# The final norm's row sums taken from the feature tiles instead of the turned tiles, with one root for all tokens

## The chip, the cores and the metric

The kernel runs on one core of one Trainium2 chip. The metric is the device time of one execution in microseconds (us), as the median of several runs. A profiled execution is one more run, with a trace; its span goes from the first to the last instruction.

## What is computed

One decoder layer on 512 tokens of width 1024 (attention with three dilated windows, then a gated ConvFFN), everything in float32, followed by a last RMSNorm over each token's 1024 features. Only the end matters here:

```python
def rms_norm(x, gain):
    xf = x.astype(jnp.float32)
    y = xf * lax.rsqrt(jnp.mean(xf * xf, axis=-1, keepdims=True) + EPS)
    return (y * gain.astype(jnp.float32)).astype(x.dtype)
...
        x = x + g2[:, None, :] * conv_ffn(h, ffn_w_up[i], ffn_conv_w[i], ffn_conv_b[i], ffn_w_down[i])
    return rms_norm(x, norm_final)
```

## The kernel before

The residual `xT` lies turned in SBUF: 8 tiles of 128 features (partitions) by 512 tokens. The down projection is the last large product. It runs over 22 strips of the hidden width, and for every strip over the 8 output tiles `o`; each output tile has a PSUM bank of its own, `y_bank(o)`. Each product is made of three passes with split operands (`wl` with `act_h`, `wh` with `act_h`, `wh` with `act_l`). The order of all instructions on every engine is written out by hand, and semaphores alone tie the engines together.

**TensorE's tail.** The last two strips are taken tile by tile (L1047 to L1049), so that output tile 0 is done first and tile 7 last; each counts up `y_done`. Between the tiles stand the turns back: `BACK_AT` says behind which tile which turned tile `m` is made. Turned tile `m` has 128 tokens (token group `m % 4`) and 512 features (half `m // 4`), and goes into `y_bank(m)`, which is free by then. It takes four 128x128 transposes (L1055). Turned tiles 0 to 3 (features 0 to 511) stand behind tiles 4, 5 and 6; turned tiles 4 to 7 all stand behind tile 7, since they need `xT` tile 7: 4 and 5 its first 256 tokens, 6 and 7 its last 256.

**VectorE's tail.** `add_ffn(o)` (L1775) adds tile `o` to `xT` (`x2_done`), tile 7 in two halves of 256 tokens. `add_gain(m)` (L1793) multiplies turned tiles 0 to 3 with the gain row `nfin` into `out_n`, without the root. `last_root(pair)` (L1783 to L1788) makes the root of two token groups; `output(m)` (L1798) multiplies turned tiles 4 to 7 with root and gain at once.

**ScalarE's tail.** For each turned tile `m` one Square with a row sum (L1312, `ssq_o`), which needs the tile turned; after turned tiles 5 and 7 a square root of two columns (L1318); last, `out_n` parts 2 and 3 are scaled by their root (L1323). GpSimd does the same for parts 0 and 1 (L680).

**The stores.** All eight stores of 128 tokens by 512 features (256 KB each) are issued by SyncE (L619) in the order 4, 0, 5, 1, 6, 2, 7, 3, each after a wait for its part; then SyncE waits until all have landed.

So the token groups 0 and 1 get their root as soon as turned tiles 4 and 5 are squared, and groups 2 and 3 get theirs in a second round.

Of the kernel before, what the change touches and what calls it, by code (L numbers as in the profile page):

```python
# [21 lines left out]
ACT = mybir.ActivationFunctionType  # L22
# [58 lines left out]
def decoder_layer(nc, x, c, w_ada, b_ada, norm_mix, norm_ffn, attn_w_in, attn_w_out,  # L81
# [11 lines left out]
    with ctx:  # L93
        def tensor(scope, name, shape, dt=F32):
            return scope.enter_context(nc.sbuf_tensor(name, shape, dt))

        def sem(name):
            return ctx.enter_context(nc.semaphore(name))
# [23 lines left out]
        ssq_o = tensor(ctx, "ssq_o", [P, NT, 2])  # L122


        scope_a = ExitStack()
# [63 lines left out]
        scope_e = ExitStack()  # L189
        out_n = tensor(scope_e, "out_n", [P, NT, D])  # L190
        nfin = tensor(scope_e, "nfin", [P, D])
        scope_e.close()

        banks = [ctx.enter_context(nc.psum_tensor(f"bank{i}", [P, T], F32)) for i in range(8)]
# [51 lines left out]
        x2_done, nat_done, ssq_done, rstd_step, out_done, root_o_done, stored = (  # L246
            sem("x2_done"), sem("nat_done"), sem("ssq_done"), sem("rstd_step"), sem("out_done"),
            sem("root_o_done"), sem("stored"))
        out_pool_done = sem("out_pool_done")
        gained, out_a_done = sem("gained"), sem("out_a_done")  # L250

        block = ctx.enter_context(nc.Block())
# [243 lines left out]
        def _(sp):  # L496
# [116 lines left out]
                sp.dma_start(down_raw(k % FRING).rearrange("p t n -> p (t n)"), w_down[k]).then_inc(fraw_in[k % FRING], 16)  # L613
            sp.wait_ge(prod_done, PRODUCTS * (FT - PLAIN))
            sp.dma_start(nfin[:], norm_final.partition_broadcast(P)).then_inc(nfin_in, 16)
            for i in range(NT):
                for m, done, value in ((i + NT, out_done, i + 1), (i, (out_pool_done, out_a_done)[i // 2], i % 2 + 1)):
                    sp.wait_ge(done, value)
                    sp.dma_start(out_rows[i][:, T * (m // 4):T * (m // 4 + 1)], out_part(out_n, m)).then_inc(stored, 16)  # L619
            sp.wait_ge(stored, 16 * 2 * NT)  # L620


# [1 line left out]
        def _(pool):  # L624
# [44 lines left out]
            for f in range(PLAIN + 1, FT):  # L669
                w = f % 2  # L670
                one, two = up_raw(w)
                for a, other_block, came in ((0, two[:, HK:KT], fraw_in[2 * w + 1]), (1, one[:, 0:HK], fraw_in[2 * w])):
                    pool.wait_ge(sum_in[w][a], 16 * sum_uses(f))
                    pool.wait_ge(came, loads_of(f, w, None))
                    nc.gpsimd.dma_start(sums[:, 4 * w + 2 * a], other_block, accum_op=ALU.add).then_inc(sum_added[w][a], 16)

            pool.wait_ge(gained, 2)
            pool.wait_ge(rstd_step, 3)
# [7 lines left out]
        def _(pe):  # L686
# [357 lines left out]
            for o in range(KT):  # L1044
                for k in (FT - 2, FT - 1):
                    slot = k % FRING
                    nc.tensor.matmul(y_bank(o)[:], wl[:, slot, o], act_h[:, slot], start=False, stop=False)  # L1047
                    nc.tensor.matmul(y_bank(o)[:], wh[:, slot, o], act_h[:, slot], start=False, stop=False)
                    last = nc.tensor.matmul(y_bank(o)[:], wh[:, slot, o], act_l[:, slot], start=False, stop=(k == FT - 1))  # L1049
                last.then_inc(y_done, 1)  # L1050
                for m in BACK_AT.get(o, ()):

                    pe.wait_ge(x2_done, 4 if m < 4 else KT if m < 6 else KT + 1)
                    for q in range(4):
                        last = nc.tensor.transpose(y_bank(m)[:, P * q:P * (q + 1)],  # L1055
                                                   xT[:, 4 * (m // 4) + q, P * (m % 4):P * (m % 4 + 1)], ident[:])
                    last.then_inc(nat_done, 1)
# [3 lines left out]
        def _(act):  # L1061
# [244 lines left out]
            downs(act, down)  # L1306

            nc.scalar.activation(warm[:, 1:2], ones[:, 0:1], ACT.Sqrt)
            for m in range(2 * NT):
                act.wait_ge(nat_done, m + 1)  # L1310

                nc.scalar.activation(out_part(out_n, m), y_bank(m)[:], ACT.Square,  # L1312
                                     accum_out=ssq_o[:, m % 4, m // 4:m // 4 + 1]).then_inc(ssq_done, 1)
                if m in (5, 7):
                    pair = (m - 5) // 2
                    act.wait_ge(rstd_step, 2 + 3 * pair)
                    lo = 2 * NT + 2 * pair
                    nc.scalar.activation(root[:, 2, lo:lo + 2], root[:, 1, lo:lo + 2], ACT.Sqrt).then_inc(root_o_done, 1)  # L1318
            for i in (2, 3):

                act.wait_ge(gained, NT)
                act.wait_ge(rstd_step, 6)
                nc.scalar.activation(out_part(out_n, i), out_part(out_n, i), ACT.Copy,  # L1323
                                     scale=root[:, ROOT_STEPS, 2 * NT + i:2 * NT + i + 1]).then_inc(out_a_done, 1)


        @block.vector
        def _(dve):
# [449 lines left out]
            def last_root(pair):  # L1778

                lo = 2 * NT + 2 * pair  # L1780
                at = slice(2 * pair, 2 * pair + 2)
                dve.wait_ge(ssq_done, NT + 2 * (pair + 1))
                nc.vector.tensor_tensor(root[:, 0, lo:lo + 2], ssq_o[:, at, 0], ssq_o[:, at, 1], ALU.add).then_inc(rstd_step, 1)  # L1783
                dve.wait_ge(rstd_step, 3 * pair + 1)
                nc.vector.tensor_scalar(root[:, 1, lo:lo + 2], root[:, 0, lo:lo + 2], 1.0 / D, EPS, ALU.mult, ALU.add
                                        ).then_inc(rstd_step, 1)
                dve.wait_ge(root_o_done, pair + 1)
                nc.vector.reciprocal(root[:, ROOT_STEPS, lo:lo + 2], root[:, 2, lo:lo + 2]).then_inc(rstd_step, 1)  # L1788
                dve.wait_ge(rstd_step, 3 * pair + 3)

            def add_gain(m):
                dve.wait_ge(ssq_done, m + 1)
# [3 lines left out]
            def output(m):  # L1796

                nc.vector.scalar_tensor_tensor(out_part(out_n, m), y_bank(m)[:],  # L1798
                                               root[:, ROOT_STEPS, 2 * NT + m % 4:2 * NT + m % 4 + 1],
                                               nfin[:, T * (m // 4):T * (m // 4 + 1)], ALU.mult, ALU.mult  # L1800
                                               ).then_inc(out_done, 1)
# [40 lines left out]
```

## Time and profile before

| | before |
|---|---|
| median of 3 runs | 950.43 us (950.26 to 952.1) |
| the profiled execution | 950.68 us, its span 948.9 us |
| TensorE busy in the span | 925.9 us (98%) |
| VectorE, ScalarE, GpSimd busy | 577.3, 445.7, 51.3 us |
| mean granted TensorE clock | 0.996 |

The busy shares average over stages of very different kinds. TensorE is never idle for long until the last product of output tile 7 starts at 937.08 us; behind that come 11.8 us in which the other engines and the stores set the time.

### The profile page before, as it was taken

Reading aid. Unit: us, or ns where it says so; the run is one execution under the profiler, and the core shown is the slowest. Engines: PE = TensorE matmul, PEld = TensorE weight load, DVE = VectorE, ACT = ScalarE, POOL = GpSimd, SP = SyncE. Lnnn points to the kernel's source line nnn. Section 1 sums busy time; section 2 is a strip of 40 time slices with the busy share of each in tenths; the row PEclk is TensorE's granted clock in tenths of the full one; section 3 lists DMA queues with packets and bytes.
Section 4 is the critical chain, followed back from the end, with each engine's and each line's share of the span. In section 5 each row is a group of like instructions: output and inputs, shape, how many; then the busy total and the mean of one; then the engine's idle time right before and its main releaser. Section 6 shows DMA issues by size and latency. Waiting matters only on the chain.

```text
span 948.9 us, 16326 instructions
## 1 busy us (share of the span) xinstructions
PE 925.9 (98%) x5828; PEld 796.2 (84%) x5828; DVE 577.3 (61%) x1269; ACT 445.7 (47%) x804; POOL 51.3 (5%) x75
## 2 busy tenths in 40 slices
PE   8999999999999999999999999999999999999996
PEld 6688887888888888888888779789999999888884
DVE  3445565736736557357365657798888888633325
ACT  7244534435444445353443445655656666523222
POOL 2000000000000000000000000411211111000000
PEclk9999999999999999999999999999999999999999
DMA  9865341443324324334142103278888885532302
GB/s 303 254 191 164 111 134 47 132 133 111 120 79 132 111 58 130 121 111 146 53 134 81 54 26 98 77 163 191 185 181 193 185 199 144 166 101 88 111 1 89
DMA packets 166516, 121.19 MB, mean 128 GB/s; under 512 B 4662, under 2 KB 149198, under 8 KB 166478
## 3 DMA queue, kind: packets, MB, share of 16 engines
q1 hardware_dynamic: 161088, 111.17, 39.1%
q0 software_dynamic: 5184, 9.44, 6.7%
q8 instruction: 23, 0.38, 0.2%
q14 instruction: 15, 0.12, 0.0%
q10 hardware_dynamic: 206, 0.08, 0.0%
HBM read 109.13 MB, written 2.10 MB: 117 GB/s over the span
## 4 chain that ended last, share of the span: by engine, by line
PE 89%; DVE 5%; ACT 2%; POOL 1%; DMA 1%; issue 1%; SPq 1%; DVEq 0%; ACTq 0%
PE bank L781 14%; PE bank L783 13%; PE bank L782 13%; PE bank L986 7%; PE bank L989 6%; PE bank L988 6%; PE bank L1035 4%; PE bank L1037 4%; PE bank L1036 4%; PE bank L863 3%; PE bank L839 3%; PE bank L806 1%; PE bank L799 1%; PE bank L821 1%; PE bank L872 1%; PE bank L874 1%
## 5 line engine op out<-in xcount | busy, mean ns | idle before, releaser
L1382 DVE TENSOR_TENSOR wl<-raw,wh 128x1024 fp32r<-128x1024 f32 (+1 forms) x127 | 150.1, 1183 | 168.6 <-ACT wh L1093 168.0
L781 PE MATMUL bank<-hh,wl 128*128 128x512 f32 x544 | 218.1, 401 | 0.0
L783 PE MATMUL bank<-hl,wh 128*128 128x512 f32 x544 | 212.4, 390 | 0.0
L782 PE MATMUL bank<-hh,wh 128*128 128x512 f32 x544 | 212.0, 390 | 0.0
L1093 ACT ACTIVATE wh<-raw 128x1024 fp32r<-128x1024 f32 (+1 forms) x127 | 130.2, 1026 | 63.3 <-PE bank L1037 50.9
L781 PEld LDWEIGHTS bank<-hh,wl 128*128 128x128 f32 x544 | 102.4, 188 | 23.8 <-issue 3.5
L783 PEld LDWEIGHTS bank<-hl,wh 128*128 128x128 f32 x544 | 102.1, 188 | 22.2
L782 PEld LDWEIGHTS bank<-hh,wh 128*128 128x128 f32 x544 | 102.3, 188 | 19.4
L1164 ACT ACTIVATE probs<-probs,nmax 128x256 f32<-128x256 f32 (+1 forms) x128 | 61.8, 484 | 66.7 <-DVE nmax L1458 66.7
L986 PE MATMUL bank<-th,wl 128*128 128x256 f32 x304 | 85.1, 280 | 1.9 <-ACT p_copy L1250 0.9
L988 PE MATMUL bank<-th,wh 128*128 128x256 f32 x304 | 84.9, 279 | 0.0
L989 PE MATMUL bank<-tl,wh 128*128 128x256 f32 x304 | 84.9, 279 | 0.0
L986 PE MATMUL bank<-fh,wl 128*128 128x256 f32 x228 | 63.8, 280 | 0.0
L988 PE MATMUL bank<-fh,wh 128*128 128x256 f32 x228 | 63.7, 279 | 0.0
L989 PE MATMUL bank<-fl,wh 128*128 128x256 f32 x228 | 63.6, 279 | 0.0
L1035 PE MATMUL bank<-act_h,wl 128*128 128x512 f32 x160 | 63.1, 395 | 0.0
L1037 PE MATMUL bank<-act_l,wh 128*128 128x512 f32 x160 | 62.7, 392 | 0.0
L1036 PE MATMUL bank<-act_h,wh 128*128 128x512 f32 x160 | 62.1, 388 | 0.0
L986 PEld LDWEIGHTS bank<-th,wl 128*128 128x128 f32 x304 | 57.1, 188 | 2.3 <-ACT p_copy L1250 1.1
L988 PEld LDWEIGHTS bank<-th,wh 128*128 128x128 f32 x304 | 57.1, 188 | 0.0
L989 PEld LDWEIGHTS bank<-tl,wh 128*128 128x128 f32 x304 | 57.1, 188 | 0.0
L1093 ACT ACTIVATE wh<-sums 128x1024 fp32r<-128x1024 f32 x38 | 40.3, 1061 | 32.6 <-PE bank L989 29.0
(220 smaller groups left out, 1611.9 us busy)
## 6 DMA issues: line engine op xcount, KB each, us to landing
raw<-in_attn_w_in SPq DMA_DIRECT2D x72, 512.0 KB, 3.8
ada_raw<-in_w_ada SPq DMA_DIRECT2D x16, 1024.0 KB, 6.0
raw<-in_ffn_w_up SPq DMA_DIRECT2D x25, 512.0 KB, 4.2
sums<-in_ffn_w_up SPq DMA_DIRECT2D x36, 256.0 KB, 3.8
raw<-in_ffn_w_down SPq DMA_DIRECT2D x17, 512.0 KB, 3.3
sums<-raw POOLq DMA_DIRECT2D x27, 256.0 KB, 4.9
ada<-in_w_ada SPq DMA_DIRECT2D x16, 256.0 KB, 6.7
raw<-in_attn_w_out SPq DMA_DIRECT2D x8, 512.0 KB, 4.2
```

What stands on the lines that cost most here:

```text
L781: nc.tensor.matmul(bank[:], wl[:, slot, t], xh[:, t], start=(t == 0), stop=False)
L782: nc.tensor.matmul(bank[:], wh[:, slot, t], xh[:, t], start=False, stop=False)
L783: last = nc.tensor.matmul(bank[:], wh[:, slot, t], xl[:, t], start=False, stop=(t == KT - 1))
L986: nc.tensor.matmul(bank[:, 0:HALF], low, xh[:, t], start=(fresh and t == 0), stop=False, skip_group_check=True)
L988: nc.tensor.matmul(bank[:, 0:HALF], high, xh[:, t], start=False, stop=False, skip_group_check=True)
L989: last = nc.tensor.matmul(bank[:, 0:HALF], high, xl[:, t], start=False, stop=(final and t == HK - 1), skip_group_check=True)
L1035: nc.tensor.matmul(y[:], wl[:, u, o], act_h[:, u], start=start, stop=False)
L1036: nc.tensor.matmul(y[:], wh[:, u, o], act_h[:, u], start=False, stop=False)
L1037: last = nc.tensor.matmul(y[:], wh[:, u, o], act_l[:, u], start=False, stop=False)
L1093: nc.scalar.activation(dst, src, ACT.Copy).then_inc(done, 1)
L1164: last = nc.scalar.activation(tile, tile, ACT.Exp, bias=nmax[:, side, b, hd:hd + 1], scale=SCORE_SCALE, accum_out=stat[:, side, b, 1, hd:h ...
L1382: nc.vector.tensor_tensor(dst, src, high.bitcast(F32), ALU.subtract).then_inc(done, 1)
```

## The change

The sums of squares no longer come from the turned tiles. ScalarE squares each feature tile of `xT` as soon as its `add_ffn` is done (`squares_o`, 7 tiles whole and tile 7 in two halves). GpSimd adds tiles 0 to 6 of them into `squares_sum`, six adds of 128x512, each of which waits for its square and for the add before it. TensorE turns sums into one number for each token with products against one column of ones: `count_squares` makes four products (one for each token group) of `squares_sum` directly behind output tile 7, and four of `squares_o` tile 7 between turned tiles 5 and 6, into columns 0 to 3 and 4 to 7 of `y_bank(0)`. VectorE adds the two with one reduction and makes one root for all 512 tokens; ScalarE takes one square root of four columns. Stores 2 and 3 are issued on ScalarE's queue, the other six on SyncE's.

```diff
-            for i in range(NT):
-                for m, done, value in ((i + NT, out_done, i + 1), (i, (out_pool_done, out_a_done)[i // 2], i % 2 + 1)):
-                    sp.wait_ge(done, value)
-                    sp.dma_start(out_rows[i][:, T * (m // 4):T * (m // 4 + 1)], out_part(out_n, m)).then_inc(stored, 16)
+            for m, done, value in ((4, out_done, 1), (0, out_pool_done, 1), (5, out_done, 2), (1, out_pool_done, 2),
+                                   (6, out_done, 3), (7, out_done, 4)):
+                sp.wait_ge(done, value)
+                sp.dma_start(out_rows[m % NT][:, T * (m // 4):T * (m // 4 + 1)], out_part(out_n, m)).then_inc(stored, 16)
...
+            for o in range(1, KT - 1):
+                pool.wait_ge(squared_o, o + 1)
+                if o > 1:
+                    pool.wait_ge(summed_o, o - 1)
+                nc.gpsimd.tensor_tensor(squares_sum[:], squares_o[:, 0] if o == 1 else squares_sum[:], squares_o[:, o], ALU.add
+                                        ).then_inc(summed_o, 1)
...
+                def count_squares(src, at):
+                    for q in range(NT):
+                        last = nc.tensor.matmul(y_bank(0)[:, at + q:at + q + 1], src[:, P * q:P * (q + 1)], ones[:, 0:1],
+                                                start=True, stop=True)
+                    return last
+                if o == KT - 1:
+                    pe.wait_ge(gained, 1)
+                    pe.wait_ge(summed_o, KT - 2)
+                    count_squares(squares_sum[:], 0)
                 for m in BACK_AT.get(o, ()):
+                    if m == 6:
+                        pe.wait_ge(squared_o, KT + 1)
+                        count_squares(squares_o[:, KT - 1], NT).then_inc(counted_o, 1)
...
-            for m in range(2 * NT):
-                act.wait_ge(nat_done, m + 1)
-                nc.scalar.activation(out_part(out_n, m), y_bank(m)[:], ACT.Square,
-                                     accum_out=ssq_o[:, m % 4, m // 4:m // 4 + 1]).then_inc(ssq_done, 1)
-                if m in (5, 7):
...
+            for o, tokens in [(o, slice(0, T)) for o in range(KT - 1)] + [(KT - 1, slice(0, HALF)), (KT - 1, slice(HALF, T))]:
+                act.wait_ge(x2_done, o + 1 + (tokens.start > 0))
+                nc.scalar.activation(squares_o[:, o, tokens], xT[:, o, tokens], ACT.Square).then_inc(squared_o, 1)
+            act.wait_ge(rstd_step, 2)
+            nc.scalar.activation(root[:, 2, 2 * NT:3 * NT], root[:, 1, 2 * NT:3 * NT], ACT.Sqrt).then_inc(root_o_done, 1)
...
+            for i in (2, 3):
+                act.wait_ge(out_a_done, i - 1)
+                act.dma_start(out_rows[i][:, 0:T], out_part(out_n, i)).then_inc(stored, 16)
...
-            last_root(0)
-            output(4)
-            output(5)
-            last_root(1)
-            output(6)
-            output(7)
+            last_root()
+            for m in range(4, 8):
+                output(m)
```

TensorE's instructions from the last pass of output tile 7 to the end, before (bank4 is the bank of tile 7, bank2, 6, 5 and 4 take turned tiles 4 to 7):

```order
L1049 MATMUL bank4<-act_l,wh 128x512
L1055 MATMUL bank2<-ident,xT 128x128 [waits x2_done]
L1055 MATMUL bank2<-ident,xT 128x128 x3
L1055 MATMUL bank6<-ident,xT 128x128 [waits x2_done]
L1055 MATMUL bank6<-ident,xT 128x128 x3
L1055 MATMUL bank5<-ident,xT 128x128 [waits x2_done]
L1055 MATMUL bank5<-ident,xT 128x128 x3
L1055 MATMUL bank4<-ident,xT 128x128 [waits x2_done]
L1055 MATMUL bank4<-ident,xT 128x128 x3
```

The same place now:

```order
L1058 MATMUL bank4<-act_l,wh 128x512
L1063 MATMUL bank3<-ones,squares_sum 128x1 [waits summed_o,gained]
L1063 MATMUL bank3<-ones,squares_sum 128x1 x3
L1077 MATMUL bank2<-ident,xT 128x128 [waits x2_done]
L1077 MATMUL bank2<-ident,xT 128x128 x3
L1077 MATMUL bank6<-ident,xT 128x128 [waits x2_done]
L1077 MATMUL bank6<-ident,xT 128x128 x3
L1063 MATMUL bank3<-ones,squares_o 128x1 [waits squared_o]
L1063 MATMUL bank3<-ones,squares_o 128x1 x3
L1077 MATMUL bank5<-ident,xT 128x128 [waits x2_done]
L1077 MATMUL bank5<-ident,xT 128x128 x3
```

The eight column products stand ahead of and between the turns, and the first of them waits for GpSimd's last add.

ScalarE's instructions from its table load to its last scaling, before:

```order
L1308 ACTIVATE warm<-ones 128x1
L1312 ACTIVATE out_n,ssq_o<-bank 128x512 [waits nat_done] x6
L1318 ACTIVATE root<-root 128x2 [waits rstd_step]
L1312 ACTIVATE out_n,ssq_o<-bank 128x512 [waits nat_done] x2
L1318 ACTIVATE root<-root 128x2 [waits rstd_step]
L1323 ACTIVATE out_n<-out_n,root 128x512 [waits rstd_step,gained] x2
```

The same place now, with the two stores:

```order
L1330 ACTIVATE warm<-ones 128x1
L1333 ACTIVATE squares_o<-xT 128x512 [waits x2_done] x7
L1333 ACTIVATE squares_o<-xT 128x256 [waits x2_done] x2
L1335 ACTIVATE root<-root 128x4 [waits rstd_step]
L1340 ACTIVATE out_n<-out_n,root 128x512 [waits rstd_step,gained] x2
L1344 DMA out_x<-out_n 128x512 [waits out_a_done] x2
```

The squares now wait for VectorE's additions, no longer for the turned tiles, and the two rounds of roots are one.

## Rows read from the trace of the kernel before

**Rows 1.** The page: shares of the chain that ended last.
```profile
PE 89%; DVE 5%; ACT 2%; POOL 1%; DMA 1%; issue 1%; SPq 1%; DVEq 0%; ACTq 0%
```

**Rows 2.** The chain's last pieces: start us, length us, engine, tile, line.
```profile
937.52 0.49 DVE xT L1775
...
938.05 0.67 PE bank L1055 x4
...
938.75 1.27 ACT out_n L1312 x4
...
940.05 0.17 DVE root L1783
...
940.88 1.41 DVE out_n L1798 x2
```

**Rows 3.** Timeline (start, us, engine, line, op, tiles) of SP; windows, ending in DMA share, GB/s.
```profile
941.66 4.48 SPq L619 DMA_DIRECT2D out_x<-out_n  x8
...
942.50:943.00 0.50, 0.00 (x0) 0.00 (x0) 0.23 (x2) 0.20 (x1) 0.00 (x0) 1.00 0.97 365
...
947.00:948.00 1.00, 0.00 (x0) 0.00 (x0) 0.00 (x0) 0.00 (x0) 0.00 (x0) 0.50 1.01 379
948.00:948.40 0.40, 0.00 (x0) 0.00 (x0) 0.00 (x0) 0.00 (x0) 0.00 (x0) 0.50 0.05 15
```

**Rows 4.** Timeline of DVE: additions of tiles 1, 6 and 7 (two halves).
```profile
927.46 0.75 DVE L1775 SCALAR_TENSOR_TENSOR xT<-bank,less_g,xT 128x512 f32<-128x512 f32 x1 [0.62 <-PE bank L1049]
...
935.25 0.75 DVE L1775 SCALAR_TENSOR_TENSOR xT<-bank,less_g,xT 128x512 f32<-128x512 f32 x1 [0.42 <-PE bank L1049]
...
937.52 0.88 DVE L1775 SCALAR_TENSOR_TENSOR xT<-bank,less_g,xT 128x256 f32<-128x256 f32 x2 [0.92 <-PE bank L1049]
```

**Rows 5.** ScalarE's squares of an earlier norm: durations in ns, min/median/max.
```profile
L1192 ACT ACTIVATE sq<-xT x11: 417/417/635, 564.1 to 588.2; 128x256 f32<-128x256 f32 x8, 128x512 f32<-128x512 f32 x3
```

**Rows 6.** Timeline: GpSimd's two-input adds elsewhere, and engines beside them.
```profile
590.07 0.49 ACT L1202 ACTIVATE h<-xn,mod 128x256 f32<-128x256 f32 x1
590.64 0.73 POOL L659 TENSOR_TENSOR fl<-h,fh 128x256 fp32r<-128x256 f32 x1 [4.85 <-ACT h L1202]
...
591.42 0.19 PEld L963 LDWEIGHTS bank<-fh,wl_first 128*128 128x128 f32 x1 [0.70 <-POOL fl L659]
...
601.96 1.23 DVE L1382 TENSOR_TENSOR wl<-raw,wh 128x1024 fp32r<-128x1024 f32 x1 [0.46 <-ACT wh L1093]
...
602.05 1.74 POOL L666 TENSOR_TENSOR h<-fh,fl 128x256 f32<-128x256 f32 x1
...
603.38 1.53 DVE L1654 SCALAR_TENSOR_TENSOR gate_in<-bank,cols_b,gate_in 128x511 f32<-128x511 f32 x2 [0.20 <-ACT gate_in L1233]
...
603.75 1.44 POOL L666 TENSOR_TENSOR h<-fh,fl 128x256 f32<-128x256 f32 x2
```

**Rows 7.** Timeline of GpSimd: fills of two sizes, selects without and with a wait.
```profile
1.15 0.21 POOL L628 MEMSET ones<- 128x128 f32 x1
1.29 0.53 POOL L629 MEMSET mask<- 128x512 f32 x1
...
3.35 0.28 POOL L646 TENSOR_SCALAR_AFFINE_SELECT mask<-mask 32x128 f32<-32x128 f32 x1
3.78 0.28 POOL L644 TENSOR_SCALAR_AFFINE_SELECT mask<-mask 32x128 f32<-32x128 f32 x1
```

**Rows 8.** Timeline: two column products of an earlier norm, and what follows them.
```profile
577.86 0.54 PEld L882 LDWEIGHTS bank<-ones,sq_sum 128*128 128x128 f32 x4
...
578.32 0.19 PEld L872 LDWEIGHTS bank<-oh,wl 128*128 128x128 f32 x1
...
578.52 0.16 DVE L1579 TENSOR_SCALAR root<-bank 128x2 f32<-128x2 f32 x1 [1.12 <-PE bank L882]
```

**Rows 9.** Timeline of the weight loads of the last 16 turns.
```profile
938.05 1.73 PEld L1055 LDWEIGHTS bank<-ident,xT 128*128 128x128 f32 x16 [1.01 <-DVE xT L1775]
```

**Rows 10.** Timeline: scalings of `out_n` on GpSimd.
```profile
941.04 1.36 POOL L680 TENSOR_SCALAR out_n<-out_n,root 128x512 f32<-128x512 f32 x2 [145.74 <-DVE root L1788]
```

More of the change, by code:

```diff
@@ L121, in decoder_layer @@
         root = tensor(ctx, "root", [P, ROOT_STEPS + 1, 3 * NT])
-        ssq_o = tensor(ctx, "ssq_o", [P, NT, 2])
         scope_a = ExitStack()
@@ L191, in decoder_layer @@
         nfin = tensor(scope_e, "nfin", [P, D])
+        squares_o = tensor(scope_e, "squares_o", [P, KT, T])
+        squares_sum = tensor(scope_e, "squares_sum", [P, T])
         scope_e.close()
@@ L245, in decoder_layer @@
         gate_done, gated, act_h_done, act_l_done = sem("gate_done"), sem("gated"), sem("act_h_done"), sem("act_l_done")
-        x2_done, nat_done, ssq_done, rstd_step, out_done, root_o_done, stored = (
-            sem("x2_done"), sem("nat_done"), sem("ssq_done"), sem("rstd_step"), sem("out_done"),
+        x2_done, nat_done, rstd_step, out_done, root_o_done, stored = (
+            sem("x2_done"), sem("nat_done"), sem("rstd_step"), sem("out_done"),
             sem("root_o_done"), sem("stored"))
         out_pool_done = sem("out_pool_done")
+        squared_o, summed_o, counted_o = sem("squared_o"), sem("summed_o"), sem("counted_o")
         gained, out_a_done = sem("gained"), sem("out_a_done")
@@ L1308, in _ @@
             nc.scalar.activation(warm[:, 1:2], ones[:, 0:1], ACT.Sqrt)
-            for m in range(2 * NT):
-                act.wait_ge(nat_done, m + 1)
-                nc.scalar.activation(out_part(out_n, m), y_bank(m)[:], ACT.Square,
-                                     accum_out=ssq_o[:, m % 4, m // 4:m // 4 + 1]).then_inc(ssq_done, 1)
-                if m in (5, 7):
[L1315 to L1318, printed above, removed]
+            for o, tokens in [(o, slice(0, T)) for o in range(KT - 1)] + [(KT - 1, slice(0, HALF)), (KT - 1, slice(HALF, T))]:
[3 more added lines that the diff above has]
+            nc.scalar.activation(root[:, 2, 2 * NT:3 * NT], root[:, 1, 2 * NT:3 * NT], ACT.Sqrt).then_inc(root_o_done, 1)
             for i in (2, 3):
                 act.wait_ge(gained, NT)
-                act.wait_ge(rstd_step, 6)
+                act.wait_ge(rstd_step, 3)
                 nc.scalar.activation(out_part(out_n, i), out_part(out_n, i), ACT.Copy,
                                      scale=root[:, ROOT_STEPS, 2 * NT + i:2 * NT + i + 1]).then_inc(out_a_done, 1)
+            for i in (2, 3):
+                act.wait_ge(out_a_done, i - 1)
+                act.dma_start(out_rows[i][:, 0:T], out_part(out_n, i)).then_inc(stored, 16)
         @block.vector
@@ L1776, in add_ffn, with last_root @@
                                                xT[:, o, tokens], ALU.mult, ALU.add).then_inc(x2_done, 1)
[L1778 to L1785, printed above, removed]
-                                        ).then_inc(rstd_step, 1)
-                dve.wait_ge(root_o_done, pair + 1)
-                nc.vector.reciprocal(root[:, ROOT_STEPS, lo:lo + 2], root[:, 2, lo:lo + 2]).then_inc(rstd_step, 1)
-                dve.wait_ge(rstd_step, 3 * pair + 3)
+            def last_root():
+                at = slice(2 * NT, 3 * NT)
+                dve.wait_ge(counted_o, 1)
+                nc.vector.tensor_reduce(root[:, 0, at], y_bank(0)[:, 0:2 * NT].rearrange("p (a q) -> p q a", a=2), AX.X, ALU.add
+                                        ).then_inc(rstd_step, 1)
+                dve.wait_ge(rstd_step, 1)
+                nc.vector.tensor_scalar(root[:, 1, at], root[:, 0, at], 1.0 / D, EPS, ALU.mult, ALU.add).then_inc(rstd_step, 1)
+                dve.wait_ge(root_o_done, 1)
+                nc.vector.reciprocal(root[:, ROOT_STEPS, at], root[:, 2, at]).then_inc(rstd_step, 1)
+                dve.wait_ge(rstd_step, 3)
             def add_gain(m):
-                dve.wait_ge(ssq_done, m + 1)
+                dve.wait_ge(nat_done, m + 1)
                 nc.vector.tensor_tensor(out_part(out_n, m), y_bank(m)[:], nfin[:, T * (m // 4):T * (m // 4 + 1)], ALU.mult
@@ L1796, in output @@
             def output(m):
+                dve.wait_ge(nat_done, m + 1)
                 nc.vector.scalar_tensor_tensor(out_part(out_n, m), y_bank(m)[:],
```

## Prediction

> **What bounds the kernel now.** The page first: the chain of work that ended last lies 89% on TensorE [rows 1], but the change leaves TensorE's products alone up to the last pass of output tile 7. So I read the last 12 us, and the chain's last pieces first [rows 2]. The addition of half a tile 7 at 937.52 lets the turns start at 938.05; four turns, then two Squares on ScalarE with their row sums, end at 940.02; the small steps of the root run from 940.05 to 940.88, where the first output starts. I call this moment R: 940.88 before.
>
> Behind R the chain as printed goes over the second root and VectorE's last output. The stores tell another story. The first is issued at 941.66, 0.78 behind R. The windows over the stores show the 16 DMA engines at a share of 0.97 already in the window from 942.50, and still at 1.01 in that from 947, with 365 to 379 GB/s, and done soon after 948.00 [rows 3]. That is about 5.55 us for 2.1 MB without a gap, then 0.83 us to the end of the span at 948.88. The end thus hangs on when the first store starts: 940.88 + 0.78 + 0.84 to the first data + 5.55 + 0.83 = 948.88. The second round of roots (first output from it at 943.08) is hidden: four stores, 4 x 0.69 = 2.8 us of traffic, cover the time to the fifth. **The end moves with R, one to one, as long as the stores stay fed.** What makes R is to be summed.
>
> **The change part by part.**
>
> *Squares on ScalarE.* Each `add_ffn` is followed by a Square from SBUF instead of from PSUM. The same form elsewhere takes 0.42 us for 256 tokens and up to 0.635 for 512 [rows 5]; I take 0.62, and 0.04 for the handover. VectorE's additions end at 928.21 for tile 1, at 936.00 for tile 6, and for tile 7 by 938.40 [rows 4]. So the Squares of tiles 1 and 6 are there at 928.87 and 936.66, those of tile 7 at about 938.9. ScalarE has nothing else to do then: free. `add_gain` now waits for the turned tile instead of its Square, which is earlier, but it stands behind the same `add_ffn` in VectorE's order: nothing.
>
> *Six adds on GpSimd.* ScalarE to GpSimd costs 0.08 (590.56 to 590.64), and an add of 128x256 takes 0.73 to 0.74 [rows 6]. For 512 columns no row exists. Bounds: 0.73, if size cost nothing, and 1.48, twice the row. Fills of 128 and 512 columns took 0.21 and 0.53 [rows 7], so about 0.10 of an instruction is fixed; 0.10 + 2 x 0.64 = 1.38, near the upper bound, and this I take. An add also waits for the one before: 3.63 to 3.78 is 0.15 [rows 7]. The pitch is 1.53, a little over the 1.37 at which tiles come. Adds start at 928.95, 930.48, 932.01, 933.54, 935.07; the sixth could start at 936.60, but its Square with the handover is there at 936.74. It ends at 938.12. With 1.48 the row of adds falls behind: start at 937.10, end at 938.58. With 0.73 it ends at 937.47.
>
> The adds have VectorE beside them. What the trace shows: the add at 602.05 took 1.74 instead of 0.74 beside a VectorE instruction with both inputs in SBUF (601.96, `wl` from `raw` and `wh`), while the two adds from 603.75 took 1.44 together (0.74 each, overlapping a little) beside one with a PSUM input (603.38) [rows 6]. All of VectorE's instructions from 926 to 940 are of the second kind, so I add nothing. The Trainium skill says the same in "SBUF — State Buffer", section "Who interferes with whom": a VectorE instruction with two SBUF inputs contends with a GpSimd instruction that reads SBUF, one with at most one doesn't; the trace agrees, 1.74 against 0.74. Were the rule wrong for this place, the sum would be that of the slower rival below.
>
> *Wait and first column products on TensorE.* The wait stands in front of all of the last 16 turns; behind it on TensorE are turned tiles 4 to 7, and behind these all four outputs of VectorE. GpSimd to TensorE takes 0.05 (591.37 to 591.42) [rows 6]. The products can start at 938.17, where the turns started at 938.05: **+0.12**. (Bounds: TensorE is free at about 937.5, with the adds at 0.73; 938.63 with 1.48.) A column product shows as two weight loads: two products took from 577.86 to 578.32, 0.46 [rows 8]. Four take **0.92**. They reuse bank3, whose reader `add_gain(0)` is long done.
>
> *Turns of tiles 4 and 5*: eight, unchanged. 16 weight loads in 1.73 [rows 9] is 0.109 a turn, 0.87 for eight. Then four more products of `squares_o` tile 7, whose wait (938.9) is over: 0.92. From the end of the loads to the reader VectorE's takes 0.20 (578.32 to 578.52) [rows 8].
>
> So the reduction starts at 938.17 + 0.92 + 0.87 + 0.92 + 0.20 = 941.08. Before, the first small step started at 940.05, since turns and Squares overlapped: only four turns stood ahead of the first Square, and the Squares of m = 4 and 5 took 1.27 [rows 2]. **+1.03.**
>
> *The root.* The reduction reads 8 columns from PSUM; the nearest is the 0.16 of a two-column read there [rows 8]. Then the same steps as before for four columns instead of two, all at their fixed price: 0.83 in all as before [rows 2], R = 941.91. One root fewer saves VectorE about 0.7 us, but behind R, where nothing waits for it.
>
> *Outputs and stores.* VectorE needs 1.41 for two outputs [rows 2], a pitch of 0.66: its four end at R + 0.75, 1.41, 2.07 and 2.74. GpSimd ends its two at R + 0.85 and R + 1.52 (0.16 to the start, 1.36 for both [rows 10]). ScalarE's two end by about R + 1.4, now without a second root ahead. SyncE issues at about 0.45 each (8 took 4.48 with their waits [rows 3]), ScalarE's queue takes two. The traffic needs the n-th store issued by R + 0.78 + 0.69 (n-1): 0.78, 1.47, 2.16, 2.85, 3.54 and so on. Issued are 4 and 0 by 1.25, store 2 by 1.5, 5 by 1.7, 3 by 2.0, 1 by 2.2, and 6 and 7 by 2.9. No gap, as before, and so no gain from issuing on two queues: 5.55 us of traffic stay.
>
> Sum on the profiled execution: 950.68 (1.8 us around the span) + 1.03 = 951.71. The median lies 0.25 below the profiled run: 950.43 + 1.03 = **951.5**. With the bounds of the add: 0.73 lets the products start at 937.5, R + 0.4, 950.8; 1.48 gives R + 1.5, 951.9.
>
> **The rivals.**
>
> *Slower: the adds fall behind.* If an add with its wait takes longer than the pitch of the tiles, the delay grows six times. The end of the sixth is then 928.95 + 5 x (d + 0.15) + d = 929.70 + 6d. The time passes +1.9 us (0.2%) when the add ends at 939.0, d = 1.55. With 1.74 (the slow row [rows 6], as it stands) it ends at 940.14: +2.0 over my sum, 953.5. With 2.24 (1.74 and the second half of a tile at 0.5) it is 943.1: 956.5. For it: no row for 512 columns, and 1.55 is only 5% over twice the row. Against: the fixed part, and the undisturbed adds.
>
> *The stores drain faster from two queues.* No row has stores on two queues. I allow a tenth less traffic time than the 5.55 us of one queue (an allowance of mine, not a reading): 0.5 us less, 951.0. Against: the share of 1.01 with one queue [rows 3], which leaves no idle time to win. The Trainium skill ("Trainium Kernel Development and Optimization", section "Key Constraints") says that queues of different engines run on the same 16 DMA engines and that issuing from several saves only issue time; no run here shows it yet.
>
> *The change does what it is worded to do, a root earlier.* If the column products cost nothing on TensorE, the reduction could start at 938.17 + 0.87 + 0.20 = 939.24, R = 940.07, 0.81 earlier than before: 949.6. Against: they stand in the one order of the same engine, and two of them pushed the next load back by 0.46 [rows 8]. Even this stays within 0.2%.
>
> *The column products cost more:* a group of eight loads costs 8 x 0.19 = 1.5 instead of 0.92 if loads did not overlap: +1.2 more, 952.7.
>
> **How the numbers follow.** My forecast (951.1 to 951.9) 0.65; adds slower than 1.5: 0.15, half of it beyond 953; faster stores 0.08; free products 0.03; dearer products 0.06; something unseen 0.03. A measurement of this kernel can tell about 0.2%, 1.9 us, from no change. Faster by more needs R before 939.0, which no case gives: 0.02. Slower by more (over 952.3) takes in the slow adds, most of the dear products, and some of the unseen: 0.18. The same: 0.80. The range 950.5 to 953.0 leaves out the worst adds, free products and part of the unseen.
>
> **What would show it.** Right: GpSimd's sixth add ends at about 938.1, TensorE's first column product starts within 0.1 of that and the eighth of its turns at 940; the reduction is at 941.1; the first store at 942.7; the DMA share is full for 5.5 us; the span is 949.9. Wrong, if the adds take over 1.5 us each or start only at the end of the one before with their Squares long done; if DMA traffic lasts under 5.2 us or has gaps; or if the span moves otherwise than the first store.

## The result: 1.6% slower, and not in the final norm

| | before | changed |
|---|---|---|
| median | 951.26 us (4 runs, 950.26 to 952.48) | 966.77 us (4 runs, 966.22 to 967.95) |
| ratio, 95% interval | | 1.0158 (1.014 to 1.0176) |
| span of the profiled execution | 948.9 us | 965.4 us |
| mean granted TensorE clock | 0.996 | 0.995 |

The forecast was 951.5, with 953.0 as its upper end. The kernel came out 15 us slower. The tail of the changed kernel shows where these 15 us are not. First VectorE's and GpSimd's rows of the timeline (start us, length us, engine, line, operation, tiles, and in brackets the idle time before and who ended it):

```profile
953.13 0.88 DVE L1795 SCALAR_TENSOR_TENSOR xT<-bank,less_g,xT 128x256 f32<-128x256 f32 x2 [0.92 <-PE bank L1058]
953.92 1.28 DVE L1812 TENSOR_TENSOR out_n<-bank,nfin 128x512 f32<-128x512 f32 x2
956.56 0.17 DVE L1802 TENSOR_REDUCE root<-bank 128x4 f32<-128x8 f32 x1 [1.36 <-PE bank L1063]
...
957.42 2.73 DVE L1818 SCALAR_TENSOR_TENSOR out_n<-bank,root,nfin 128x512 f32<-128x512 f32 x4
...
944.51 1.29 POOL L683 TENSOR_TENSOR squares_sum<-squares_o 128x512 f32<-128x512 f32 x1 [136.58 <-ACT squares_o L1333]
945.94 4.16 POOL L683 TENSOR_TENSOR squares_sum<-squares_sum,squares_o 128x512 f32<-128x512 f32 x3
...
952.36 1.28 POOL L683 TENSOR_TENSOR squares_sum<-squares_sum,squares_o 128x512 f32<-128x512 f32 x1 [0.49 <-ACT squares_o L1333]
```

The same stretch on TensorE: the last pass of output tile 7, column products, turns.

```profile
952.70 0.39 PE L1058 MATMUL bank<-act_l,wh 128*128 128x512 f32 x1
953.78 1.02 PE L1063 MATMUL bank<-ones,squares_sum 128*128 128x1 f32 x8 [0.69 <-POOL squares_sum L683]
954.66 1.07 PE L1077 MATMUL bank<-ident,xT 128*128 128x128 f32 x8
955.57 0.95 PE L1063 MATMUL bank<-ones,squares_o 128*128 128x1 f32 x8
956.39 1.07 PE L1077 MATMUL bank<-ident,xT 128*128 128x128 f32 x8
```

And the stores: SyncE's row, then windows whose last two numbers are DMA share and GB/s.

```profile
958.20 4.47 SPq L621 DMA_DIRECT2D out_x<-out_n  x6
...
959.50:960.00 0.50, 0.00 (x0) 0.00 (x0) 0.50 (x1) 0.00 (x0) 0.00 (x0) 0.50 1.02 373
964.00:964.50 0.50, 0.00 (x0) 0.00 (x0) 0.00 (x0) 0.00 (x0) 0.00 (x0) 0.50 0.95 381
```

The addition of tile 7 starts at 953.13, where it was 937.52 before [rows 4]: **15.61 us are lost before the final norm's own part begins.** From that addition to the first output it is 957.42 - 953.13 = 4.29, before 940.88 - 937.52 = 3.36 [rows 2]: **+0.93**, forecast +1.03. From the first output to the end of the span it is 965.4 - 957.42 = 8.0, as before.

So the tail came out close to the forecast, and the 15.6 us come from stages whose instructions the diff doesn't touch. TensorE's products of the attention and the feed-forward show it. Groups by line, before and after (x instructions | busy us, mean ns of one | idle before):

```profile
L781 PE MATMUL bank<-hh,wl 128*128 128x512 f32 x544 | 218.1, 401 | 0.0
L783 PE MATMUL bank<-hl,wh 128*128 128x512 f32 x544 | 212.4, 390 | 0.0
L988 PE MATMUL bank<-th,wh 128*128 128x256 f32 x304 | 84.9, 279 | 0.0
```

```profile
L790 PE MATMUL bank<-hh,wl 128*128 128x512 f32 x544 | 220.5, 405 | 0.0
L792 PE MATMUL bank<-hl,wh 128*128 128x512 f32 x544 | 215.3, 396 | 0.0
L997 PE MATMUL bank<-th,wh 128*128 128x256 f32 x304 | 86.0, 283 | 0.0
```

Each pass takes 4 to 6 ns more. The durations overlap, so what a pass really costs is the time from its start to the next one's. Nine starts in a row in the attention, the same passes, before and then after:

```profile
149.97 0.39 PE L781 MATMUL bank<-hh,wl 128*128 128x512 f32 x1
...
151.78 0.39 PE L783 MATMUL bank<-hl,wh 128*128 128x512 f32 x1
```

```profile
150.00 0.40 PE L790 MATMUL bank<-hh,wl 128*128 128x512 f32 x1
...
151.87 0.40 PE L792 MATMUL bank<-hl,wh 128*128 128x512 f32 x1
```

1.81 us for eight steps before, 1.87 after. It isn't the clock: windows over the same 95 us of the down projection show a granted clock of 1.00 (the higher level, 2.4 GHz) in both kernels and a TensorE that is busy all the time, but 417 passes before and 409 after (second number and its count; the clock is the third number from the end):

```profile
830.00:925.00 95.00, 95.00 (x417) 77.95 (x416) 29.21 (x32) 26.80 (x34) 0.00 (x0) 1.00 0.23 76
```

```profile
830.00:925.00 95.00, 95.00 (x409) 76.30 (x408) 35.77 (x42) 30.55 (x40) 0.00 (x0) 1.00 0.30 101
```

Windows over the whole run up to 925 us show a granted clock of 1.00 in both kernels, but for 0.98 from 450 to 560 us, again in both. (The two windows above don't cover quite the same passes, since the changed kernel is late by then.) Worked out from the start times of all matmul records (median step, and the sum of all steps, which takes in the few waits):

| products | passes | step before, ns | after, ns | sum before, us | after, us |
|---|---|---|---|---|---|
| attention projections, `wl`/`wh` by `hh`/`hl`, 512 columns | 1632 | 227, 227, 227 | 232, 232, 235 | 381.6 | 390.0 |
| up projection, `wl`/`wh` by `th`, `fh` and so on, 256 columns | 1596 | 116, 117, 117 | 120, 120, 120 | 188.7 | 193.7 |
| down projection, by `act_h`/`act_l`, 512 columns | 528 | 232, 226, 229 | 234, 234, 234 | 122.0 | 124.3 |
| output projection, by `oh`/`ol`, 512 columns | 96 | 227, 227, 226 | 235, 234, 235 | 26.5 | 27.3 |
| the same, 256 columns | 192 | 120, 120, 120 | 117, 117, 117 | 23.4 | 23.1 |

8.4 + 4.9 + 2.2 + 0.8 - 0.3 = 16.0 us. All other steps and waits of TensorE up to the addition of tile 7 are together 0.4 us shorter, which leaves the 15.6.

What the two kernels don't share in these stages is not an instruction but an address. The diff takes out `ssq_o`, a tile of 32 bytes in each partition. SBUF tiles are laid one behind the other, and `ssq_o` was the last one ahead of all tiles of the stages: each of them now lies 32 bytes lower. The addresses below are those that the built programs give their tiles. `hh` went from 181888 to 181856, `th` from 71328 to 71296, `act_h` from 181952 to 181920, while `xT`, `wh` (30848) and `wl` (47232), which stand ahead, stayed.

### The profile page after: what moved, and what is told of

Same layout as the page of the kernel before. It is cut to its first block, busy times and chain, and to the rows that moved or that the text cites. A ratio compares the mean times of both kernels' runs of the same rounds, so it can differ in the third digit from the quotient of the medians.

```text
span 965.4 us, 16360 instructions
## 1 busy us (share of the span) xinstructions
PE 942.1 (98%) x5844; PEld 801.8 (83%) x5844; DVE 577.9 (60%) x1266; ACT 446.8 (46%) x796; POOL 59.0 (6%) x81
## 4 chain that ended last, share of the span: by engine, by line
PE 89%; DVE 5%; ACT 2%; POOL 1%; DMA 1%; SPq 1%; issue 1%; DVEq 0%; ACTq 0%
PE bank L790 14%; PE bank L792 13%; PE bank L791 13%; PE bank L995 7%; PE bank L998 6%; PE bank L997 6%; PE bank L1044 4%; PE bank L1045 4%; PE bank L1046 4%; PE bank L872 3%; PE bank L848 3%; PE bank L815 1%; PE bank L808 1%; PE bank L830 1%; PE bank L881 1%; PE bank L883 1%
## 5 line engine op out<-in xcount | busy, mean ns | idle before, releaser
L790 PE MATMUL bank<-hh,wl 128*128 128x512 f32 x544 | 220.5, 405 | 0.0
L792 PE MATMUL bank<-hl,wh 128*128 128x512 f32 x544 | 215.3, 396 | 0.0
L791 PE MATMUL bank<-hh,wh 128*128 128x512 f32 x544 | 215.1, 395 | 0.0
```

The costliest lines, as they stand in the source:

```text
L790: nc.tensor.matmul(bank[:], wl[:, slot, t], xh[:, t], start=(t == 0), stop=False)
L791: nc.tensor.matmul(bank[:], wh[:, slot, t], xh[:, t], start=False, stop=False)
L792: last = nc.tensor.matmul(bank[:], wh[:, slot, t], xl[:, t], start=False, stop=(t == KT - 1))
```

## The experiments

Each group of experiments was run beside fresh runs of the kernel before on the same chip, so each result is a ratio to those; steps and rows come from one profiled execution. "Difference" below is the address of a product's moving operand (512 or 256 columns wide) less that of `wl`, modulo 256; `wh` lies at the same place modulo 256 as `wl`. "Modulo 256" is what is left of the difference when whole multiples of 256 bytes are taken away.

**The changed kernel with 32 bytes given back** (`after_spaced`).

```diff
         root = tensor(ctx, "root", [P, ROOT_STEPS + 1, 3 * NT])
+        tensor(ctx, "spacer", [P, 8])
```

> The changed kernel with one unused tile of 32 B per partition put where ssq_o stood, so that every tile behind it lies at the address that it had before the change. Address theory: the 14.7 us ahead of the final norm come from the addresses alone, so the last stage's own +0.93 is all that is left: 951.2 to 952.4 us, passes of hh by wl, wh, hl by wh 227 ns apart instead of 232 to 235. Rival, that the other program (one semaphore more in use at a time, other instruction stream, GpSimd's and ScalarE's new work) slows TensorE: 966 us, as the changed kernel.

Measured: 952.84 us, before 951.42; ratio 1.0018 (0.9999 to 1.0036). The groups of passes shown are those of before to the digit, and the tail keeps its 4.29 (942.32 - 938.03):

```profile
L791 PE MATMUL bank<-hh,wl 128*128 128x512 f32 x544 | 218.1, 401 | 0.0
L793 PE MATMUL bank<-hl,wh 128*128 128x512 f32 x544 | 212.4, 390 | 0.0
...
938.03 0.88 DVE L1796 SCALAR_TENSOR_TENSOR xT<-bank,less_g,xT 128x256 f32<-128x256 f32 x2 [0.92 <-PE bank L1059]
...
942.32 2.73 DVE L1819 SCALAR_TENSOR_TENSOR out_n<-bank,root,nfin 128x512 f32<-128x512 f32 x4
```

An unused tile wins back 14 of the 15.5 us. The other program, its semaphores and its new work on ScalarE and GpSimd leave these passes as they were. (The addition of tile 7 starts at 938.03 here and at 937.52 before; 0.5 us lies well inside the spread of the executions of before, 949.21 to 955.04.)

**The kernel before, all stages 32 bytes higher** (`before_all32`) **and 64 bytes higher** (`before_all64`).

```diff
         ssq_o = tensor(ctx, "ssq_o", [P, NT, 2])
+        tensor(ctx, "spacer", [P, 8])
```

> The kernel before with one unused tile of 32 B behind ssq_o: not one instruction changes, but every tile of the stages moves up by 32 B (hh from 0 to 32 modulo 64). Address theory: 951.0 + 14.7 = about 965.5 us, with passes of 232 to 235 ns in the attention's projections. Rival (the program): 951 us, nothing moves.

> The same with 64 B: the place modulo 64 stays as before, that modulo 128 changes. If the place modulo 64 counts: 951 us and 227 ns. If that modulo 128 counts: the passes of hh change as with 32 B, or in part, some 5 to 15 us more.

Measured: 961.71 us, ratio 1.0102 (1.0081 to 1.0124), and 959.37 us, ratio 1.0082 (1.0056 to 1.0108). Not one instruction differs from the kernel before but in the addresses of its tiles. So the addresses alone slow it, and the rival (the program) is out. But 961.7 is 3.8 us short of the 965.5 expected. With 32 bytes the attention's steps are 234, as expected, yet the up projection stays at 117 to 118 ns, where the changed kernel has 120. With 64 bytes the attention's are 232, 226 and 229, the up projection's 120: the first case of that expectation, 951 us, failed, and the loss of 8 us lies in the range of the second. So the operand's place modulo 64 alone doesn't tell the step.

**Only `hh` and `hl` 32 bytes higher** (`before_hh32`).

```diff
+        tensor(scope_a, "spacer", [P, 8])
         hh = tensor(scope_a, "hh", [P, KT, T], F32R)
```

> The kernel before with the 32 B put just ahead of hh and hl, the moving operands of the attention's projections: all else stays. If the moving operand's place counts: the 1632 passes of 512 columns rise from 227 to 232 to 235 ns, +8 to +11 us, 960 us, and the passes of the feed-forward stay at 116 to 117 and 226 to 232 ns. If something else in the shifted region counts: no change.

Measured: 961.5 us, ratio 1.0104 (1.0062 to 1.0146); the profiled execution 958.8. 234 ns for `hh`, all others untouched (`th` 116 to 117, `act_h` 232, 226, 229):

```profile
L782 PE MATMUL bank<-hh,wl 128*128 128x512 f32 x544 | 220.5, 405 | 0.0
...
L989 PE MATMUL bank<-th,wh 128*128 128x256 f32 x304 | 84.9, 279 | 0.0
```

So the attention's products go by their own operands. Two readings were left: the moving operand's own address counts, or its distance from the weights, which had not moved in any run so far.

**The weights 32 bytes higher, the moving operands not** (`before_weights32`), **and weights and all behind them together** (`before_weights_and_all32`). In the first, the small tiles between `wl` and the stages (`ident` to `root`) move up with the weights; the products told here read none of them.

```diff
+        ssq_o = tensor(ctx, "ssq_o", [P, NT, 2])
         wh = tensor(ctx, "wh", [P, FRING, KT, P], F32R)
...
         root = tensor(ctx, "root", [P, ROOT_STEPS + 1, 3 * NT])
-        ssq_o = tensor(ctx, "ssq_o", [P, NT, 2])
```

```diff
+        tensor(ctx, "spacer", [P, 8])
         wh = tensor(ctx, "wh", [P, FRING, KT, P], F32R)
```

> The kernel before with ssq_o (32 B) allocated ahead of wh and wl instead of behind root: the split weights move up by 32 B, the moving operands of all products stay where they are. So far the passes of 512 columns read, by the moving operand's address less the weights' modulo 256: 0 gives 227 ns, 64 gives 229, 32 gives 234, 96 and 224 give 233, 128 gives 232; those of 256 columns: 0 gives 120, 32 gives 116.5, 64 gives 118, 96 gives 120. Theory of the difference of both operands: hh by wl becomes 224, 233 ns; th by wl becomes 0, 120 ns; act_h by wl becomes 32, 234 ns; in all +15 us, about 966. Rival, that the moving operand's own address counts: 227, 116.5 and 229 stay, 951 us.

> The kernel before with 32 B ahead of wh, so that weights and moving operands move together. Theory of the difference: all passes stay, 227, 116.5 and 229 ns, 951 us. Rival, the moving operand's own address: as with 32 B on all but the weights, 234, 118 and 233 ns, 961.7 us.

Measured: 965.65 us, ratio 1.0162 (1.0132 to 1.0191), and 951.04 us, ratio 1.0004 (0.9991 to 1.0018). This pair decides it. In the first, no moving operand of these products has moved, and yet it is the changed kernel's loss again (the difference is for each product the same as there), with the same busy time in each group shown:

```profile
L781 PE MATMUL bank<-hh,wl 128*128 128x512 f32 x544 | 220.5, 405 | 0.0
L783 PE MATMUL bank<-hl,wh 128*128 128x512 f32 x544 | 215.3, 396 | 0.0
...
L988 PE MATMUL bank<-th,wh 128*128 128x256 f32 x304 | 86.0, 283 | 0.0
```

In the second, every operand of these products has moved, and nothing is lost:

```profile
L782 PE MATMUL bank<-hh,wl 128*128 128x512 f32 x544 | 218.1, 401 | 0.0
L784 PE MATMUL bank<-hl,wh 128*128 128x512 f32 x544 | 212.4, 390 | 0.0
```

**One product at a time** (`before_forms32`, `before_act32`). The kernel before has pads of its own around `th`, `tl`, `fh` and `fl`.

```diff
-        tensor(scope_f, "ahead_of_forms", [P, 8])
...
-        tensor(scope_f, "behind_forms", [P, 8])
+        tensor(scope_f, "behind_forms", [P, 16])
```

```diff
-        tensor(scope_f, "behind_forms", [P, 8])
+        tensor(scope_f, "behind_forms", [P, 16])
...
-        tensor(scope_n, "ahead_of_t32", [P, 16])
+        tensor(scope_n, "ahead_of_t32", [P, 24])
```

> The kernel before with the 32 B that stand ahead of th, tl, fh, fl moved behind them: only these four move, down by 32 B (difference 0 to the weights). Expected: the 1596 passes of 256 columns from 116.5 to 120 ns, +4.9 us as between the two kernels (188.7 to 193.7 us in all), 956 us; the passes of hh stay at 227 ns.

> The kernel before with 32 B more behind the forms, so that act_h and act_l (and t32, h2 and the first up strips' weights) move up by 32 B, difference 96 to the weights. Expected: the 528 passes of the down projection from a mean of 229 to 233 ns, +2.1 us, 953.5 us; hh at 227 and th at 116.5 ns.

Measured, one execution each: 956.52 and 954.67 us beside 950.67 (949.12 to 952.0). The up projection's steps are 120 (its sum 193.7 us, as in the changed kernel) in the first; the down projection's 238, 230 and 232 in the second (its sum 124.2 us, beside 124.3 in the changed kernel, though there the difference is 32 and here 96), with `hh` at 227 in both. Together with the 8.4 us of `hh` these are the three large parts of the loss.

**Is 0 the best difference for `act_h` too?** (`before_act0`, one execution)

```diff
-        tensor(scope_f, "behind_forms", [P, 8])
+        tensor(scope_f, "behind_forms", [P, 56])
...
-        tensor(scope_n, "ahead_of_t32", [P, 16])
+        tensor(scope_n, "ahead_of_t32", [P, 64])
```

> The kernel before with act_h and act_l moved up by 192 B, nothing else. Theory of the difference: 227 ns instead of 229 in the down projection, about 950 us where before is 951.

Measured: 949.15 us beside 950.73 (23 runs, 948.54 to 954.65); one execution can't tell this from no change, but the steps can: 226, 227 and 227, where they were 232, 226 and 229. The 227 ns of `hh` at difference 0 carried over to another product.

All that was read, by difference:

| difference | 512 columns, ns (three passes) | read in | 256 columns, ns | read in |
|---|---|---|---|---|
| 0 | 227, 227, 227 | `hh`, before; `act_h`, act0; `fh` by `wl`, changed and forms32 | 120 | `th`, changed, forms32, weights32 |
| 32 | 234, 234, 234 | `hh`, all32 and hh32; `act_h`, changed; `fh` by `wl`, before | 116 to 117 | `th`, before |
| 64 | 232, 226, 229 | `hh`, all64; `act_h`, before | 117 to 118 | `th`, all32 |
| 96 | 238, 230 to 231, 231 to 232 | `act_h`, all32 and act32 | 120 | `th`, all64 |
| 128 | 232, 232, 232 | `act_h`, all64 | not read | |
| 192 | 234, 233, 233 | `fh` by `wl_first`, forms32 | not read | |
| 224 | 232, 232, 235 | `hh`, changed; `fh` by `wl_first`, before, changed | 117 | `oh`, changed |

Where the three passes differ, the same three values can stand in another order at the same difference: `act_h` at 64 is 232, 226, 229 in before and 229, 232, 226 in `after_spaced`. The mean of the three, 229, is what the difference tells.

The products of `fh` with 512 columns (96 passes) test the table once more, since half of them take their weights from `wl` and `wh`, and half from `wl_first` and `wh_first`, which lie elsewhere (190144 and 181952, difference 224 in before). Before, both halves are slow (32 and 224), 232 to 235 ns. In `before_forms32`, where `fh` and `fl` move against both pairs of weights, to 0 and 192, the first half falls to 227 and the second stays at 233 to 234; the groups show it too (before, then `before_forms32`):

```profile
L978 PE MATMUL bank<-fh,wh_first 128*128 128x512 f32 x16 | 6.3, 395 | 0.0
...
L978 PE MATMUL bank<-fh,wh 128*128 128x512 f32 x16 | 6.3, 395 | 0.0
```

```profile
L977 PE MATMUL bank<-fh,wh_first 128*128 128x512 f32 x16 | 6.3, 394 | 0.0
L976 PE MATMUL bank<-fh,wl 128*128 128x512 f32 x16 | 6.2, 390 | 0.0
L977 PE MATMUL bank<-fh,wh 128*128 128x512 f32 x16 | 6.2, 390 | 0.0
```

**The tail with its first root earlier** (`two_roots`), on the spaced kernel. The column products of token groups 0 and 1 come first and give a root of their own; those of groups 2 and 3, into the bank of output tile 1, and a second root follow behind turned tiles 4 and 5.

```diff
                 if o == KT - 1:
                     pe.wait_ge(gained, 1)
                     pe.wait_ge(summed_o, KT - 2)
-                    count_squares(squares_sum[:], 0)
+                    count_squares(squares_sum[:], 0, 0)
+                    pe.wait_ge(squared_o, KT)
+                    count_squares(squares_o[:, KT - 1], NT, 0).then_inc(counted_o, 1)
                 for m in BACK_AT.get(o, ()):
                     if m == 6:
                         pe.wait_ge(squared_o, KT + 1)
-                        count_squares(squares_o[:, KT - 1], NT).then_inc(counted_o, 1)
+                        pe.wait_ge(gained, 2)
+                        count_squares(squares_sum[:], 0, 1)
+                        count_squares(squares_o[:, KT - 1], NT, 1).then_inc(counted_o, 1)
...
-            last_root()
-            for m in range(4, 8):
-                output(m)
+            for pair in range(2):
+                last_root(pair)
+                output(4 + 2 * pair)
+                output(5 + 2 * pair)
```

> The changed kernel with the 32 B spacer, its column products in two parts: those of token groups 0 and 1 (four products, 0.9 us) ahead of turned tiles 4 and 5, those of groups 2 and 3 (into the bank of output tile 1) behind them, and two roots again. Taking the tail's own theory (the end moves with the first root): the products start where the changed kernel's do, 0.15 behind the place of the first turn before; 0.9 for four products plus 0.2 and 0.85 for the root put R 1.8 us ahead of the changed kernel's and 0.8 us ahead of the kernel before: 950.2 us where before is 951.0. Rival, that VectorE's last output or the second root becomes the bound: no gain over the spaced kernel (+0.93, 951.9).

Measured: 950.99 us, before 950.73; ratio 1.0003 (0.9987 to 1.0018). The times can't settle half a microsecond, so this goes by the trace. VectorE, and the last column products ahead of the turns on TensorE:

```profile
937.71 0.88 DVE L1802 SCALAR_TENSOR_TENSOR xT<-bank,less_g,xT 128x256 f32<-128x256 f32 x2 [0.92 <-PE bank L1059]
938.50 1.27 DVE L1819 TENSOR_TENSOR out_n<-bank,nfin 128x512 f32<-128x512 f32 x2
939.70 0.15 DVE L1809 TENSOR_REDUCE root<-bank 128x2 f32<-128x4 f32 x1
...
940.52 1.41 DVE L1825 SCALAR_TENSOR_TENSOR out_n<-bank,root,nfin 128x512 f32<-128x512 f32 x2
...
938.80 0.58 PE L1064 MATMUL bank<-ones,squares_o 128*128 128x1 f32 x4
939.24 1.07 PE L1082 MATMUL bank<-ident,xT 128*128 128x128 f32 x8
```

The first output comes 2.81 behind the addition, against 3.36 before and 4.29 in the changed kernel: the new order gives back 1.5 us, and against the kernel before 0.55 is won, not 0.8. The reduction has no idle time ahead of it: it stands behind `add_gain(3)`, which ends when it starts. TensorE goes over from these products to the turns at 939.24; in the changed kernel the reduction started 0.17 behind the same point (956.56 - 956.39). So by estimate it could have started at 939.41 and was held until 939.70 by VectorE's own order, which is the missing quarter of a microsecond. The end of the span is at 948.6, 8.1 behind that first output.

**Both together** (`two_roots_act0`): the same with the pads of `before_act0`.

> The same with act_h and act_l moved up by 192 B, so that their addresses less those of wh and wl are 0 modulo 256, as those of hh are. Theory of the difference: the 528 passes of the down projection come from a mean of 229 ns to 227 ns, 1.1 us less, 949.1 us. Rival (the number does not carry over from hh): 229 ns or more, 950 to 952 us.

Measured: 950.0 us, ratio 0.9991 (0.9976 to 1.0005); the profiled span is 947.3, and the steps of the down projection are 227, 226 and 227. The steps are as the theory of the difference has them, but the expected 949.1 us is not shown: the spans of this kernel's executions run from 946.1 to 952.1, and the interval takes in no change.

**All stores on one queue** (`spaced_one_queue`), on the spaced kernel.

```diff
             for m, done, value in ((4, out_done, 1), (0, out_pool_done, 1), (5, out_done, 2), (1, out_pool_done, 2),
-                                   (6, out_done, 3), (7, out_done, 4)):
+                                   (6, out_done, 3), (2, out_a_done, 1), (7, out_done, 4), (3, out_a_done, 2)):
...
-            for i in (2, 3):
-                act.wait_ge(out_a_done, i - 1)
-                act.dma_start(out_rows[i][:, 0:T], out_part(out_n, i)).then_inc(stored, 16)
```

> The changed kernel with the 32 B spacer and all eight stores on SyncE's queue, in the order of the kernel before. If the stores' traffic is bound by the DMA engines: from the first output to the end of the span 8.0 us, as with two queues. If two queues had helped: 8.2 or more.

Measured, one execution: its first output is at 942.00, its span ends at 950.0: 8.0, as with two queues (7.98 in `after_spaced`).

```profile
942.00 2.72 DVE L1816 SCALAR_TENSOR_TENSOR out_n<-bank,root,nfin 128x512 f32<-128x512 f32 x4
...
942.77 4.47 SPq L622 DMA_DIRECT2D out_x<-out_n  x8
```

In these two traces the two stores on ScalarE's queue gained and cost nothing.

## Why the prediction was wrong

The step that failed is in its first paragraph: "the change leaves TensorE's products alone up to the last pass of output tile 7". I took a removed tile declaration for a change without a cost and gave it no line in the sum. In its place the runs showed that it moves the moving operands against the weights and makes the passes of the large products 2 to 8 ns longer: 15.6 us, 15 times the +1.03 of the sum. None of the rivals had it ("something unseen" stood at 0.03); the range held only mechanisms of the last 12 us. The kernel did offer a sign: among its tiles stand small ones that nothing reads (`ahead_of_forms` and `behind_forms` of 32 bytes, `ahead_of_t32` of 64). Such pads in a tuned kernel suggest that places matter to it, though what they were put there for is not on record, and a diff that takes 32 bytes from ahead of them moves everything that they place.

The mechanisms of the tail were right, point by point (times of the changed kernel less 15.61):

| step | predicted | trace after |
|---|---|---|
| Square of 512 tokens from SBUF | 0.62 | 0.63 |
| add of 128x512 on GpSimd | 1.38 (0.73 to 1.48) | 1.28 |
| from one queued add's start to the next | 1.53 | 1.43 (945.94 - 944.51) |
| end of the sixth add | 938.12 | 938.03 (953.64) |
| first column product's turn on TensorE | 938.17 | 938.17 (953.78) |
| four column products | 0.92 | 0.88 (954.66 - 953.78) and 0.82 (956.39 - 955.57) |
| start of the reduction | 941.08 | 940.95 (956.56) |
| first output R | 941.91 | 941.81 (957.42) |
| from R to the end of the span | 8.0 | 8.0 |

*The adds:* right in length, inside the bounds. The forecast had the first five queued one behind the other and only the sixth waiting for its Square; in the trace the first four are queued, and the fifth and the sixth each wait 0.49 for their Squares, released by ScalarE. All six took 1.28 to 1.29 or, in the run of three, 4.16 together, so no contention with VectorE showed. *The column products* stood ahead of and between the turns at the full price on TensorE. *Stores:* the end moves with the first output one to one, 8.0 us behind it in before, changed, spaced and one queue (8.1 in `two_roots`). The Trainium skill ("Trainium Kernel Development and Optimization", section "Key Constraints") says that issuing from several engines saves only issue time; 8.0 against 7.98 agrees. *Both slower rivals* (slow adds, dear column products) had the right sign by luck alone: neither happened.

With the address effect taken away (`after_spaced`) the change gives 1.0018 (0.9999 to 1.0036), that is +1.7 us give or take 1.7, beside +1.03 forecast and +0.93 in the trace. Whether the new final norm is faster has, by the trace, the answer no: it gives the first root 0.9 later, since eight column products in two groups and four more turns stand ahead of it on TensorE, where before four turns and two Squares did. The times alone can't tell it from no change.

## What to carry to other kernels

Read a removed, added or resized tile as a move of all tiles allocated behind it, and when a diff changes the layout, compare the addresses of matmul operands before the times; an unused tile of the same size is a cheap control experiment. When a whole stage that the diff doesn't touch moves by a per cent or two, look at the step between successive instructions at full clock first: it separates a slower instruction from a new wait at once. When you read a step, group it by both operands and not by line: one line of code can draw its weights from two tiles, as that of `fh` does. A tail's gain is only as large as the next queue allows: in `two_roots` VectorE's own order took about a third of the 0.8 us expected.

## What the runs showed of the hardware

*A pass's step depends on where its two operands lie to each other.* With weights loaded for every pass (128x128, float32r) and 512 columns streamed, the step was 226 to 238 ns at a granted clock of 1.00, and its mean over the three passes (227 to 234) followed the difference of the two addresses, to within 2 ns, in every product and run read; for 256 columns it was 116 to 120 ns. 32 bytes decide 3% (227 against 234). The order isn't the same for both widths: 0 is the best read for 512 columns and, with 96, the worst for 256. While one pass streams, the weights of the next are loaded (the rows of the loads lie beside those of the passes), so TensorE's two reads may get in each other's way in SBUF; that is only argued and not shown, since no run separated the load from the pass. The Trainium skill, "SBUF — State Buffer", section "Who interferes with whom", gives TensorE two independent read ports, one for the moving operand and one for the weight load, and says that it never waits on anyone. No run here tests it against other engines; for its own two operands, 227 against 234 ns is a step that depends on both places together, which independent ports alone don't explain.

*Open:* why the step depends on the difference, and whether the pattern repeats every 256 bytes at every difference. Two readings agree with it: 0 gave 227 ns both where the whole difference is a multiple of 512 (`hh`) and where it is 256 over one (`act_h` in `before_act0`), and 32 gave 234 for `hh` in `before_hh32` and for `fh` by `wl_first` in `before_act0` in the same way.

*GpSimd's add of two float32 tiles of 128x512* took 1.28 us, and 0.15 us went by between one and the next that waits for it (945.94 - 944.51 - 1.28). *A float32 product by one column* shows as two pairs of a weight load and a pass, 0.11 us each (eight pairs in 954.66 - 953.78 = 0.88).
